# A hybrid attention and RWKV-7 block: fill, first step and mask order of the chunked recurrence stage

## The reference

```python
def step(S, inp):
    r_t, w_t, k_t, v_t, a_t, b_t = inp
    sa = jnp.einsum('bhij,bhj->bhi', S, a_t)
    S = (S * w_t[:, :, None, :] + sa[..., None] * b_t[:, :, None, :]
         + v_t[..., None] * k_t[:, :, None, :])
    return S, jnp.einsum('bhij,bhj->bhi', S, r_t)
...
_, y = lax.scan(step, S0, seq_in)
...
g = jax.nn.sigmoid(xg @ g1) @ g2
...
return jnp.einsum('btd,de->bte', y * g, w_o)
```

## Time and profile before

| | |
|---|---|
| median of 3 runs | 1500.68 us (1496.58 to 1503.44) |
| the profiled execution's own time | 1501.69 us |
| its span, first to last instruction | 1500.0 us |
| mean granted PE clock | 0.985 of 2.4 GHz |
| chunk stage within the span | 876.4 to about 1057 us |
| step 1 begins (`l_products(4)` on PE) | 936.8 us |
| DVE starts `small_blocks(0)`, once its lanes have landed | 885.4 us |
| SP has issued the g2 loads | 890.5 us |
| busy over the span: PE / DVE / ACT / POOL | 95% / 69% / 49% / 6% |

### The profile page before, as it was taken

The page is one execution under the profiler, slowest core; times in us unless marked ns, Lnnn a source line. Parts: engine busy times, 40 slices in busy tenths (PEclk is TensorE's granted clock), DMA queues, the critical chain, the costliest instruction groups (busy, mean ns, idle before and its releaser), DMA issues.

```text
span 1500.0 us, 30264 instructions
## 1 busy us (share of the span) xinstructions
PE 1429.8 (95%) x12891; PEld 1315.4 (88%) x12891; DVE 1029.7 (69%) x1463; ACT 740.7 (49%) x1071; POOL 95.2 (6%) x122
## 2 busy tenths in 40 slices
PE   6999999999999999998999986999799999999997
PEld 5998898999999999998999775888367998899986
DVE  5666567588843787577968775786678883488732
ACT  4555465454532455458578542443455552255422
POOL 3010011000030000000000141110000000000010
PEclk9999999999999999999999997999999999999998
DMA  4212221423433333555322233332332343333331
GB/s 131 64 58 64 65 64 57 113 85 99 123 88 88 92 104 96 141 156 195 89 61 78 85 75 57 57 62 44 111 99 85 104 119 106 95 87 111 87 97 56
DMA packets 283990, 136.78 MB, mean 91 GB/s; under 512 B 65449, under 2 KB 278593, under 8 KB 283601
## 3 DMA queue, kind: packets, MB, share of 16 engines
q1 hardware_dynamic: 283552, 134.77, 32.6%
q10 hardware_dynamic: 304, 0.08, 0.0%
HBM read 124.33 MB, written 10.49 MB: 90 GB/s over the span
## 4 chain that ended last, share of the span: by engine, by line
PE 78%; DVE 11%; ACT 6%; DMA 3%; issue 2%; SPq 0%; DVEq 0%; ACTq 0%
PE psg L1883 26%; PE psx L1724 13%; PE psg L1724 11%; PE psg L2689 9%; PE psg L591 2%; DVE w_lo L137 2%; PE psx L591 2%; PE psg L619 2%; PE psg L675 1%; ACT rest_hi L331 1%; DVE rest_lo L430 1%; DVE sum_lo L447 1%; PE psx L3398 1%; ACT rest L317 1%; ACT rest L323 1%
## 5 line engine op out<-in xcount | busy, mean ns | idle before, releaser
L133 ACT ACTIVATE w_hi<-w_raw 128x1024 fp32r<-128x1024 f32 (+1 forms) x122 | 142.0, 1165 | 209.6 <-PE psg L1883 147.9
L1883 PE MATMUL psg<-mid_hi_l,w_hi 128*128 128x264 f32 (+1 forms) x720 | 232.8, 323 | 2.9 <-DVE w_lo L137 2.0
L1883 PE MATMUL psg<-mid_lo_l,w_hi 128*128 128x264 f32 (+1 forms) x720 | 231.6, 322 | 0.0
L1883 PE MATMUL psg<-mid_hi_l,w_lo 128*128 128x264 f32 (+1 forms) x720 | 231.0, 321 | 0.0
L137 DVE TENSOR_TENSOR w_lo<-w_raw,w_hi 128x1024 fp32r<-128x1024 f32 (+1 forms) x121 | 165.0, 1364 | 77.7 <-ACT w_hi L133 77.1
L1883 PEld LDWEIGHTS psg<-mid_hi_l,w_hi 128*128 128x128 f32 x720 | 135.3, 188 | 14.7 <-DVE w_lo L137 2.6
L1883 PEld LDWEIGHTS psg<-mid_lo_l,w_hi 128*128 128x128 f32 x720 | 135.3, 188 | 10.5 <-issue 0.2
L1883 PEld LDWEIGHTS psg<-mid_hi_l,w_lo 128*128 128x128 f32 x720 | 135.4, 188 | 10.3
L2689 PE MATMUL psg<-x_hi,w_hi 128*128 128x264 f32 (+1 forms) x320 | 99.8, 312 | 7.9 <-DVE w_lo L137 7.9
L2689 PE MATMUL psg<-x_lo,w_hi 128*128 128x264 f32 (+1 forms) x320 | 98.8, 309 | 0.0
L2689 PE MATMUL psg<-x_hi,w_lo 128*128 128x264 f32 (+1 forms) x320 | 98.6, 308 | 0.0
(11 more groups left out here) (518 smaller groups left out, 4324.2 us busy)
## 6 DMA issues: line engine op xcount, KB each, us to landing
w_raw<-in_w_ffn_out_dram SPq DMA_DIRECT2D x40, 704.0 KB, 4.7
w_raw<-in_w_qkv_dram SPq DMA_DIRECT2D x24, 512.0 KB, 3.7
w_raw<-in_w_rkv_dram SPq DMA_DIRECT2D x24, 512.0 KB, 3.9
x_raw_l<-in_w_ffn_in_dram SPq DMA_DIRECT2D x18, 512.0 KB, 4.1
x_raw_l<-in_w_ffn_in_dram SPq DMA_DIRECT2D x36, 256.0 KB, 4.7
w_raw<-in_w_ffn_in_dram SPq DMA_DIRECT2D x16, 512.0 KB, 3.9
y_raw_l<-in_w_ffn_in_dram SPq DMA_DIRECT2D x16, 512.0 KB, 4.0
y_raw_l<-in_w_ffn_in_dram SPq DMA_DIRECT2D x32, 256.0 KB, 4.6
```

Of the source, the lines that this page charges most:

```text
L133: k.nc.scalar.activation(k.w_hi[j][:, 0:kt, :], k.raw[j][:, 0:kt, :], ACT.Copy).then_inc(k.hi_ready[j].h, 1)
L1883: done = k.nc.tensor.matmul(self.bank(i, c), w[:, t, :], x, start=t == 0 and n == 0, stop=t == count - 1 and n == 2)
```

## The change

It reorders instructions. On SP `keep_low(2)` goes from behind `fetch_inverse(1)` to ahead of `keep_inverse(0)`, and `fetch_lanes(2)` between `keep_inverse(0)` and `fetch_inverse(0)`; every `keep_low(n)` from chunk 2 on waits for one lane load more. On ACT `values_turned(0, 0)` goes ahead of `decays(2)`, `lower(2)` and `decays(3)` ahead of the g2 split, `av_out(0, 0)` behind it. On DVE `products(2)` and `keys(0, 0)` go ahead of `small_blocks(0)`; step 0 gets an order of its own (`first_step`); in the later steps `products(c + 4)` goes between the two mask halves. On PE the order of the fill changes, 36 of the filler matmuls go and 16 come, `quads(1, 0)` goes ahead of `chain_u(0)` and `quads(1, 1)` right behind it. No arithmetic is changed.

```diff
@@ -2992,7 +2992,7 @@
             def keep_low(n):
                 sp.wait_ge(low_r.h, n + 1)
                 if n >= 2:
-                    sp.wait_ge(lane_in.h, 16 * (n - 1))
+                    sp.wait_ge(lane_in.h, 16 * n)
                 for half in range(2):
                     sp.dma_start(by_heads(k.low_kept[n % 2], half), low[n % 3][half_rows(half), :, :]).then_inc(low_out.h, 16)
 
@@ -3032,16 +3032,16 @@
             sp.dma_start(r.g_raw[:, 0, :, :], g2.src(0, 0)).then_inc(g_in.h, 16)
             for at in range(0, P, G_REST):
                 sp.dma_start(r.g_raw[at:at + G_REST, 1, :, :], g2.src(0, 1)).then_inc(g_in.h, 16)
+            keep_low(2)
             sp.wait_ge(inv_in.h, 64)
             for n in range(CHUNKS):
                 if 1 < n < CHUNKS - 1:
                     keep_low(n + 1)
                     fetch_lanes(n + 1)
                 keep_inverse(n)
+                if n == 0:
+                    fetch_lanes(2)
                 fetch_inverse(n)
-                if n == 1:
-                    keep_low(2)
-                    fetch_lanes(2)
 
             sp.wait_ge(quad.h, 2 * CHUNKS)
             for j in range(2):
@@ -3060,6 +3060,8 @@
 
             def lower(n):
                 act.wait_ge(lps.h, n + 1)
+                if n == 3:
+                    act.wait_ge(low_out.h, 32)
                 nc.scalar.activation(low[n % 3][:], l_ps, ACT.Copy).then_inc(low_r.h, 1)
 
             def keys_turned(n, p):
@@ -3128,15 +3130,15 @@
             decays(1)
             lower(0)
             keys_turned(0, 0)
+            values_turned(0, 0)
             decays(2)
             lower(1)
-            values_turned(0, 0)
+            lower(2)
+            decays(3)
             end_decay(0, 0)
-            av_out(0, 0)
             act.wait_ge(g_in.h, (1 + P // G_REST) * 16)
             nc.scalar.activation(r.g_hi[:], r.g_raw[:], ACT.Copy).then_inc(g_split.h, 1)
-            lower(2)
-            decays(3)
+            av_out(0, 0)
             steps(act, step)
 
         def gpsimd(pool):
@@ -3284,6 +3286,26 @@
                 nc.vector.tensor_tensor(ch.state[:], ch.state[:], w_end[q][:].broadcast_to([P, KT, C]),
                                         ALU.mult).then_inc(state_r.h, 1)
 
+            def first_step(n, p, q):
+                keys(n, 0)
+                reads(n, p, 0)
+                products(3)
+                keys(n, 1)
+                reads(n, p, 1)
+                grow(q, 0)
+                small_blocks(2)
+                next_t(n)
+                dve.wait_ge(g_split.h, 1)
+                nc.vector.tensor_tensor(r.g_lo[:], r.g_raw[:, 0], r.g_hi[:, 0].bitcast(F32), ALU.subtract)
+                next_xt(n, p, 0)
+                next_xs(n, p)
+                last_blocks(2)
+                next_xt(n, p, 1)
+                nc.vector.tensor_tensor(r.g_hi[C:P, 1], r.g_raw[C:P, 1], r.g_hi[C:P, 1].bitcast(F32),
+                                        ALU.subtract).then_inc(g_split.h, 1)
+                products(4)
+                small_blocks(3)
+
             def step(c, n, q, prep):
                 p = 1 - q
                 dve.wait_ge(av_r.h, c + 1)
@@ -3293,47 +3315,38 @@
                         .then_inc(wt_r.h, 1)
                 else:
                     nc.vector.tensor_scalar(wt[:], av[q][:], -1.0, None, ALU.mult).then_inc(wt_r.h, 1)
-                    grow(q, c)
-                    products(3)
-                    dve.wait_ge(g_split.h, 1)
-                    nc.vector.tensor_tensor(r.g_lo[:], r.g_raw[:, 0], r.g_hi[:, 0].bitcast(F32), ALU.subtract)
-                    nc.vector.tensor_tensor(r.g_hi[C:P, 1], r.g_raw[C:P, 1], r.g_hi[C:P, 1].bitcast(F32),
-                                            ALU.subtract).then_inc(g_split.h, 1)
+                    first_step(n, p, q)
+                    return
                 if not prep:
                     for j in range(2):
                         unit_lo(k, dve, u0 + j, KT)
                 if prep:
                     next_t(n)
-                if c == 0:
+                if c + 2 < CHUNKS:
+                    last_blocks(c + 2)
+                if prep:
                     next_xt(n, p, 0)
                     next_xs(n, p)
-                    small_blocks(2)
-                if c + 2 < CHUNKS:
-                    last_blocks(c + 2)
-                if prep and c:
-                    next_xt(n, p, 0)
-                    next_xs(n, p)
-                if prep and c:
                     grow(q, c)
-                if prep:
                     keys(n, 0)
                     reads(n, p, 0)
+                if c + 4 < CHUNKS:
+                    products(c + 4)
+                if prep:
                     keys(n, 1)
                     reads(n, p, 1)
                     next_xt(n, p, 1)
-                if c + 4 < CHUNKS:
-                    products(c + 4)
                 if c + 3 < CHUNKS:
                     small_blocks(c + 3)
 
             products(1)
+            products(2)
+            keys(0, 0)
             small_blocks(0)
             last_blocks(0)
-            keys(0, 0)
             keys(0, 1)
             small_blocks(1)
             last_blocks(1)
-            products(2)
             steps(dve, step)
 
         def tensor(pe):
@@ -3504,10 +3517,13 @@
                 p = 1 - q
                 if c == 0:
                     turn_bk(n)
+                    keep(8)
                     turn_v(n)
+                    keep(8)
+                    quads(n, 0)
                     chain_u(c, q)
+                    quads(n, 1)
                     chain_s(c, q)
-                    quads(n, 0)
                     l_products(3)
                     keep(8)
                     times_x(n, p, 0)
@@ -3530,7 +3546,8 @@
                     chain_y(c, q)
                 if prep:
                     times_x(n, p, 1)
-                    quads(n, 1)
+                    if c:
+                        quads(n, 1)
                     x_times(n, p, 1)
                     gate(c)
                     a_v(n, p)
@@ -3540,14 +3557,13 @@
             l_products(0)
             turn_bk(0)
             keep(8)
+            turn_v(0)
             l_products(1)
-            turn_v(0)
             quads(0, 0)
+            quads(0, 1)
+            l_products(2)
             keep(44)
-            quads(0, 1)
             a_v(0, 0)
-            keep(36)
-            l_products(2)
             steps(pe, step)
 
         stage = State()
```

## The result

The changed kernel takes 1490.71 us (median of 7 runs, 1486.15 to 1493.73), the kernel before 1503.32 us in the same comparison (7 runs, 1496.58 to 1506.64). The ratio is 0.9921 with a 95% interval of 0.9905 to 0.9938, so the kernel is 9 to 14 us faster. I had forecast 15.1 us, 1485.6 us, with a range of 1479 to 1494.

The account below looks back on a forecast made before the run. The prediction took the tensor engine (PE) and its waits in the chunk stage as the bound. Gains 11.7 + 4.6 - 0.5 - 0.7 = 15.1 us take the profiled 1501.69 to 1486.6, median 1485.6 us, range 1479 to 1494.

Parts of the forecast that it names:

- The gaps: PE's waits before l_products of steps 2 to 5, behind DVE's scaling, vanish: four of 1.15 us, 4.6 us gained.
- rival (e): Scaling moves but the step gap stays, POOL's share being last: 1.1 us a step, 1490; counted within a shared 0.10.
- The inverse's return: Shorter steps leave less time for the inverse's way through DRAM, so PE waits: 0.5 us off, between 0 and 2.0.
- The fill and step 0: times_x(1, 0) starts at 911.3 instead of 918.95, step 1 at 925.1 instead of 936.8: 11.7 us gained.
- The clock: Step 1 runs 5 us of its start at 1.2 GHz against 2.4 now: 0.7 us off, between zero and 1.3.
- Rival (c): Slower: PE idles before gate(0), then steps 1 to 3 run at 1.2 GHz; all three give 1531 us; chance 0.04.
- Rival (b): Fill gains little: keep_low(2) lands late behind g2 and holds fetch_lanes(2) and fetch_inverse(0) on SP; 1494 us; chance 0.09.
- Rival (d): Full clock throughout step 0: x_times 0.5, gate and a_v 1.5, clock 0.7 less; 1482.9 us; chance 0.05.

Follow-up runs that it names:

- the scaling alone: Kernel before with only the scaling, products(c + 4), of steps 1 to 4 moved between the mask halves: ratio 0.9976, 1500.32 us.
- the filler experiment: Kernel after with 28 more filler matmuls ahead of times_x(1, 0) and 20 ahead of gate(0): ratio 0.991, 1489.47 us.
- SP's order undone: Kernel after with keep_low(2) and fetch_lanes(2) on SP back behind fetch_inverse(1): ratio 0.9942, 1494.36 us.
- the filler runs: Kernel after with more fillers: 1489.47 us; with 28 fillers and last_blocks(2) ahead of next_t(1): 1487.97 us; that plus early g2 loads: 1490.06 us.
- the early g2 subtraction: Kernel after with g2's low-part subtraction ahead of next_t(1) on DVE: 1487.97 us, ratio 0.9897; timed once more 1489.71 us, ratio 0.992.

## Why the prediction was right, step by step

**The gaps (forecast 4.6 us).** Right in size and cause. In the kernel after steps 2 to 4 save 1.09, 1.18 and 1.21 us; the scaling alone saves 4.5 us over four steps. POOL's share ends 0.10 us before `l_products`; I had it at 0.15, so rival (e) falls too.

**The inverse's return (forecast 0.5).** Right in size, half wrong in place. I had looked for it in steps 3 and 5, behind the late loads of steps 2 and 4. It came in steps 5 and 6, which grew by 0.6 and 1.0 us, while step 7 got 0.9 shorter; net 0.7 us. In step 5 `times_x` starts 3.24 us behind the step's start instead of 2.86; the other 0.3 us are a pause in `x_times` that no wait explains. In step 6 `times_x` waited 0.57 us for the DMA, after a store that held SP for 2.10 us and not 0.67:

```profile
1001.11 2.10 SPq L3010 DMA_DIRECT2D inverse_turned_kept<-lane_xt  x1
```

```profile
1011.11 1.12 PE L3440 MATMUL psg<-xt,low 64*64 64x32 f32 x32 [0.57 <-DMA xs<-inverse_kept]
```

Before, 0.51 was lost in this way in step 7. That the size came out is partly luck: in the twelve experiments steps 5 to 7 took from 47.1 to 49.4 us together.

**The fill and step 0 (forecast 11.7, measured 8.7).** This is the term that was mis-sized. `times_x(1, 0)` was to start 34.1 us into the stage and started at 36.3. The order of the path was as I had it; its legs were longer. DVE started on chunk 0's blocks 0.3 us sooner than I had it, but `small_blocks(0)` and `last_blocks(0)` took 7.1 us and not 6.2. I had the 6.2 from chunk 2's blocks. Chunk 0's own had taken 7.1 us before the change too, from 885.4 us to this copy in DVE's timeline of the kernel before:

```profile
892.51 0.37 DVE L3232 COPY lane_xt<-lane_x 64x256 f32<-64x256 f32 x1
```

So the second store of chunk 0 went out 0.8 us late. It landed in 3.2 us, and I had taken 2.62 from one instance. The same store took 3.4 us in the scaling alone, where nothing in the fill is changed:

```profile
893.46 0.67 SPq L3010 DMA_DIRECT2D inverse_turned_kept<-lane_xt  x1
896.86 0.59 SPq L3017 DMA_DIRECT2D xt<-inverse_turned_kept  x1
```

Those of chunk 1 landed in 3.8 us, after an issue 0.4 us slower. The loads were quicker than I had them, 5.2 and 5.3 us for four with their landing instead of 5.8 and 5.4. Together that is 0.8 + 0.6 - 0.6 + 0.4 + 1.1 - 0.1 = 2.2 us. The bound that I had given, up to 1 us for each transfer, nearly held.

By the Trainium skill's fit ("DMA: Bandwidth & Descriptors", Anatomy of one DMA), which it gives for DMAs issued by GpSimd, such a store would take an estimated 2.15 us. This trace disagrees: its stores took 2.5 to 4.1 us, and the sum by that fit, for stores and loads, lay 2.9 us further off.

From there to the gate I had 10.0 us and it took 11.0: 0.8 of it because `times_x` ran at half clock (1.92 us for 1.1) and not only `x_times`. Gate and `a_v` took 3.6 us as forecast (3.8).

**The clock (forecast 0.7 off).** Step 1 ran its first 5 us at the lower clock, which was the upper case of my text (5 us against 2.4). That costs 2.2 us by the filler experiment; in step 1 without a gap before the change (the scaling alone, 16.92 against 15.7) it cost 1.2. So 1.0 us off, near the 0.7. Rival (c) falls: the clock was back at 932.

**Rival (b)** falls with SP's order undone: that cost 4.2 us, it saved nothing. Rival (d), full clock throughout, did not happen, nor in the filler runs, where the clock was at 0.50 for about 10 us; so no run tests its 2.7 us. With `times_x(1, 0)` and step 1 at full clock the whole stage gained 1.6.

**The sum.** 8.7 + 0.1 in step 1 + 3.5 in steps 2 to 4 - 0.7 = 11.6 us, all within the stage, against 15.1. The ratio gives 11.9 of 1503.3 us. Of the 5.1 us between the median that I had forecast and the measured one, 2.6 are no part of the change: the kernel before came out at 1503.3 and not at the 1500.7 from which I had counted.

## What to carry to other kernels

An instruction that fitted into a wait of the same engine cost nothing here, and the gain of the move could be costed from one profile: find the wait, its length, and what is second behind it (here POOL's share, 0.1 us away). A path made of DMA round trips is costed badly from one instance: take the spread of such landings for each leg (2.5 to 4.5 us here), and the middle for the sum. The time of a group of instructions, too, is taken from the same place in the program where the profile has it: chunk 0's blocks took 7.1 us and chunk 2's 6.2. Behind this change another 3 us saved in the stage stood in three profiles (161.0 to 161.2 us) and yet could not be told in the medians: a faster kernel is claimed from the interval and not from the stage.

## What the runs showed that I had not expected

A DVE multiply of 64x64 elements slowed threefold beside POOL's multiply in step 0, in the kernel after. DVE's rows and POOL's:

```profile
908.93 0.44 DVE L3202 TENSOR_TENSOR lane_products<-lane_low,lane_x 64x64 f32<-64x64 f32 x2
...
909.71 1.51 DVE L3206 TENSOR_TENSOR lane_products<-lane_x,lane_sums 64x64 f32<-64x64 f32 x2
```

```profile
909.75 1.36 POOL L3149 TENSOR_TENSOR bk_late<-rows,w_inv 128x512 f32<-128x512 f32 x1 [14.56 <-ACT w_inv L3059]
```

The pair took 0.44 us elsewhere. It cost nothing, as DVE waited 3.05 us right after. By the Trainium skill ("SBUF — State Buffer", SBUF: two separate sides) an operation of DVE with two SBUF inputs and one of POOL that reads SBUF take turns on a shared port, each blocking the other for its whole length; the 1.1 us that DVE lost is about one instruction of POOL, so the trace agrees.

Open is why the stores of chunk 1's inverse take 3.2 to 4.4 us in every kernel with the new fill, against 2.6 before. The DMA engines carry no more then (a share of 0.33 and 41 GB/s from 903.4 to 907.2, against 0.42 and 50 GB/s from 902.2 to 904.9 over the same stores before), and neither SP's order, nor g2's loads, nor 1 us of shift brought back the 2.6. Open is also what the 3 us saved within the stage by the early g2 subtraction turn into over the whole launch; with the stage's start scattered over 6 us from execution to execution, 3 us are below what these medians tell.
